# Attention in steps of two heads on eight cores of a Trainium2 chip, with allocations on multiples of 64 bytes

## The reference, cut to what matters

```python
q_nope, q_pe = q[..., :QK_NOPE_DIM], q[..., QK_NOPE_DIM:]      # 128 and 64
q_pe = rope(q_pe, positions)
k_pe = rope(k_rope[:, :, None, :], positions)                  # shared across heads
s = jnp.einsum('bqhd,bkhd->bhqk', qi, k).astype(jnp.float32) * scale   # over 192
s = jnp.where(mask[None, None], s, -jnp.inf)
p = jax.nn.softmax(s, axis=-1).astype(v.dtype)
return jnp.einsum('bhqk,bkhd->bqhd', p, v)
```

## Time and profile before

| | us |
|---|---|
| median of 3 runs | 2039.23 (2038.88 to 2039.92) |
| profiled execution, own time | 2044.05 |
| its span, slowest core (5) | 2042.5 |
| spans of the even cores | 1987.8 to 1994.6 |
| spans of the odd cores | 2033.2 to 2042.5 |
| core 5: TensorE busy | 1921.9 (94%) |
| VectorE / ScalarE / GpSimd busy | 1022.4 / 740.6 / 174.7 |
| DMA, mean | 86 GB/s |

### The profile page before, as it was taken

How to read it: one execution, slowest core, us unless ns; L and a number is a source line. 1 busy time by engine, 2 the same in 40 slices (tenths; PEclk the granted TensorE clock), 3 DMA queues, 4 the chain that set the end, 5 groups by cost and what they waited for, 6 DMA issues and landing times.

```text
span 2042.5 us, 26214 instructions; the slowest of 8 cores (1987.8 to 2042.5 us)
## 1 busy us (share of the span) xinstructions
PE 1921.9 (94%) x8362; PEld 788.1 (39%) x8362; DVE 1022.4 (50%) x1632; ACT 740.6 (36%) x1255; POOL 174.7 (9%) x332
## 2 busy tenths in 40 slices
PE   5999999989999999999999989999998998799996
PEld 1344544434444444444333433333343222244442
DVE  2265551463523426665565465665655575433335
ACT  3221232264321014543545333455533573311113
POOL 0021111100000100010000000110110000011110
PEclk8899999999999999999999999999999798899998
DMA  8186787744432322554222433553363001344542
GB/s 203 32 158 128 147 161 136 168 132 109 109 56 44 57 49 30 102 109 85 44 43 31 85 81 95 96 87 69 53 125 102 1 1 43 97 71 75 77 65 96
DMA packets 94686, 176.40 MB, mean 86 GB/s; under 512 B 25680, under 2 KB 46544, under 8 KB 93392
## 3 DMA queue, kind: packets, MB, share of 16 engines
q0 software_dynamic: 47232, 100.36, 31.7%
q1 hardware_dynamic: 47312, 74.26, 11.5%
HBM read 255.78 MB, written 19.14 MB: 135 GB/s over the span
## 4 chain that ended last, share of the span: by engine, by line
PE 85%; ACT 5%; DVE 5%; issue 3%; DMA 2%; SPq 1%; DVEq 0%; ACTq 0%; POOL 0%; POOLq 0%
PE ps L398 85%; ACT arena L402 4%; DVE arena L416 2%; DVE arena L406 2%; DMA arena<-wd 1%; ACT L402 1%; DMA arena<-smallc 1%; SPq L224 0%; DMA arena<-w_moR 0%; SPq L430 0%; ACTq L208 0%; DVEq L208 0%; ACT arena L422 0%; DVEq L175 0%; DVE arena L424 0%
## 5 line engine op out<-in xcount | busy, mean ns | idle before, releaser
L398 PE MATMUL ps<-arena 128*128 128x512 bf16 (+3 forms) x8362 | 1921.9, 381 | 107.2 <-DVE arena L406 35.7
L398 PEld LDWEIGHTS ps<-arena 128*128 128x128 bf16 (+1 forms) x8362 | 788.1, 98 | 1240.7 <-issue 444.4
L402 ACT ACTIVATE arena<-ps 128x512 bf16<-128x512 f32 (+2 forms) x677 | 390.7, 584 | 924.5 <-PE ps L398 868.3
L406 DVE TENSOR_TENSOR arena<-ps,arena 128x512 bf16<-128x512 f32 (+1 forms) x396 | 272.9, 691 | 694.1 <-PE ps L398 445.8
L416 DVE SCALAR_TENSOR_TENSOR arena<-ps,arena 128x512 f32<-128x512 f32 (+1 forms) x454 | 306.0, 689 | 143.8 <-PE ps L398 137.2
L406 DVE TENSOR_TENSOR arena<-arena 128x512 f32<-128x512 f32 (+10 forms) x456 | 274.7, 619 | 92.0 <-ACT arena L402 57.7
L402 ACT ACTIVATE arena<-arena 128x512 bf16<-128x512 f32 (+2 forms) x417 | 246.8, 624 | 177.8 <-PE ps L398 71.8
L416 DVE SCALAR_TENSOR_TENSOR arena<-arena 128x512 bf16<-128x512 f32 (+2 forms) x236 | 160.2, 728 | 55.9 <-ACT arena L402 36.9
L430 POOL DMA_DIRECT2D arena<-wgu x110 | 58.3, 530 | 1328.2 <-PE ps L398 1293.6
L430 POOL DMA_DIRECT2D arena<-wd x160 | 85.4, 535 | 455.4 <-PE ps L398 455.4
L422 ACT CAST arena<-ps 128x256 bf16<-128x256 f32 (+1 forms) x94 | 44.1, 477 | 114.0 <-PE ps L398 110.1
(11 more groups left out here) (15 smaller groups left out, 17.4 us busy)
## 6 DMA issues: line engine op xcount, KB each, us to landing
arena<-wgu POOLq DMA_DIRECT2D x110, 512.0 KB, 5.2
arena<-wd POOLq DMA_DIRECT2D x160, 160.0 KB, 3.3
arena<-win_s SPq DMA_DIRECT2D x46, 256.0 KB, 3.2
arena<-x SPq DMA_DIRECT2D x16, 512.0 KB, 5.5
arena<-x SPq DMA_DIRECT2D x8, 1024.0 KB, 11.3
arena<-wo_s SPq DMA_DIRECT2D x24, 256.0 KB, 2.6
arena<-xk_s SPq DMA_DIRECT2D x24, 256.0 KB, 2.6
arena<-vo_s SPq DMA_DIRECT2D x24, 256.0 KB, 2.7
```

Of the source, the lines that this page charges most:

```text
L398: S.add("pe", lambda e: e.matmul(out, lhsT=lhsT, rhs=rhs, start=start, stop=stop), reads, writes, cost=c)
L402: S.add("act", lambda e: e.activation(out=out, in_=in_, func=func, **kw), reads, writes, cost=0.17 + cols(out) * 0.00085, table=table)
L406: S.add(eng, lambda e: e.tensor_tensor(out=out, in0=in0, in1=in1, op=op), reads, writes, cost=c)
```

## The change

`attn_g` takes two heads at a time. A step is now one key block for the pair: the two 128-row matmuls of the heads, each into its own bank, then their two 64-row matmuls right behind each other, the first on the lower and the second on the upper half of the rows; then both exps (and triangle products); `stage_b` does two products and two adds. `LOOK` is 2 steps of two heads instead of 3 of one. The score banks and the product banks are taken two at a time. There are 6 slots PT in both branches, two used per step. Both tails of a pair run one after the other, one step after the pair's last product. On early cores the slots and sums are laid out anew, and RC is the same tile as ACC. The planner's cost of a matmul with 64 rows becomes half the streaming time plus 0.1 us. `take` rounds each size up to 64 bytes, so that what lies behind SC is no longer displaced by 488 bytes but by 512. The diff, with unchanged lines left out:

```diff
-    def mm(out, lhsT, rhs, start, stop, reads, writes):
-        c = cols(out) * (4.0 if out is None or lhsT.dtype == F32 else 1.0) * 0.000419
+    def mm(out, lhsT, rhs, start, stop, reads, writes, share=1.0):
+        c = cols(out) * (4.0 if out is None or lhsT.dtype == F32 else 1.0) * 0.000419 * share + (0.1 if lhsT.shape[0] == 64 else 0.0)
...
-        at[0] += nbytes
+        at[0] += -(-nbytes // 64) * 64
...
-    NPT = 6 if late else 5
+    NPT = 6
...
-        o_pt, o_acc, o_rc, o_ol = AW + 8 * K, AW + 13 * K, AW + 17 * K, AW + 21 * K
-        at[0] = max(at[0], AW + 25 * K)
+        o_pt, o_acc, o_rc, o_ol = AW + 8 * K, AW + 16 * K, AW + 16 * K, AW + 20 * K
+        at[0] = max(at[0], AW + 24 * K)
...
-    RC = [tile(("rc", i), o_rc + 2 * K * i, 2 * K) for i in range(2)]
+    RC = [tile(("rc" if late else "acc", i), o_rc + 2 * K * i, 2 * K) for i in range(2)]
...
-    LOOK = 3
+    LOOK = 2
...
-        seq = [(h, kb) for h in range(4) for kb in range(nk)]
+        seq = [(p, kb) for p in range(2) for kb in range(nk)]
...
-            b = yield from pa.get()
-            mm(ps[:, b, n0:512], KVN[:, ks], QA[:, h, n0:512], True, False, [BKVN[kb // 4], BQA[h]], [BPS[b]])
-            mm(ps[:, b, n0:512], KR[pr, ks], QPE[pr, h // 2, n0:512], False, True, [BKR[kb // 4], BQPE[h // 2]], [BPS[b]])
-            act(pt[:, n0:512], ps[:, b, n0:512], AF.Exp, [BPS[b]], [ptb], scale=sc_attn)
-            pa.put(b)
...
+            bs = yield from pa.get(2)
+            for e, b in enumerate(bs):
+                mm(ps[:, b, n0:512], KVN[:, ks], QA[:, 2 * p + e, n0:512], True, False, [BKVN[kb // 4], BQA[2 * p + e]], [BPS[b]])
+            for e, b in enumerate(bs):
+                pr = slice(64 * e, 64 * e + 64)
+                mm(ps[:, b, n0:512], KR[pr, ks], QPE[pr, p, n0:512], False, True, [BKR[kb // 4], BQPE[p]], [BPS[b]], share=0.5)
+            info[i] = []
+            for b in bs:
+                pt, ptb = PT[cnt["pt"] % NPT]
+                cnt["pt"] += 1
+                act(pt[:, n0:512], ps[:, b, n0:512], AF.Exp, [BPS[b]], [ptb], scale=sc_attn)
+                pa.put(b)
...
             if kb == 0:
-                pv[h] = yield from pa.get()
+                pv[p] = yield from pa.get(2)
+            for e in range(2):
+                pt, ptb, n0 = info[i][e]
+                b = pv[p][e]
+                mm(ps[:, b, n0:512], CTR[:, kb * 128:(kb + 1) * 128], pt[:, n0:512], kb == 0, kb == nk - 1, [BCTR[kb // 4], ptb], [BPS[b]])
+                acc, accb = ACC[e]
+                if kb == 1:
+                    p0, p0b, _ = info[i - 1][e]
+                    if n0:
+                        cp(acc[:, 0:n0], p0[:, 0:n0], [p0b], [accb])
+                    tt(acc[:, n0:512], p0[:, n0:512], pt[:, n0:512], ALU.add, [p0b, ptb], [accb])
...
-        def tail(h):
...
+        def tail(p):
+            for e in range(2):
+                rc, rcb = RC[e]
+                acc, accb = ACC[e]
...
-                    tails.append((k + 3, seq[k][0]))
+                    tails.append((k + 1, seq[k][0]))
```

More of the change, by code:

```diff
@@ L1000, in attn_g @@
         nk = 4 * (t + 1)
-        seq = [(h, kb) for h in range(4) for kb in range(nk)]
+        seq = [(p, kb) for p in range(2) for kb in range(nk)]
         pv, info, tails = {}, {}, collections.deque()
         def stage_a(i):
-            h, kb = seq[i]
+            p, kb = seq[i]
             n0 = max(0, kb - 4 * t) * 128
-            pt, ptb = PT[cnt["pt"] % NPT]
-            cnt["pt"] += 1
             ks = slice(kb * 128, (kb + 1) * 128)
-            pr = slice(64 * (h % 2), 64 * (h % 2) + 64)
-            b = yield from pa.get()
-            mm(ps[:, b, n0:512], KVN[:, ks], QA[:, h, n0:512], True, False, [BKVN[kb // 4], BQA[h]], [BPS[b]])
-            mm(ps[:, b, n0:512], KR[pr, ks], QPE[pr, h // 2, n0:512], False, True, [BKR[kb // 4], BQPE[h // 2]], [BPS[b]])
-            act(pt[:, n0:512], ps[:, b, n0:512], AF.Exp, [BPS[b]], [ptb], scale=sc_attn)
-            pa.put(b)
-            if kb >= 4 * t:
-                tt(pt[:, n0:n0 + 128], pt[:, n0:n0 + 128], TRI, ALU.mult, [ptb, BTRI], [ptb])
-            info[i] = pt, ptb, n0
+            bs = yield from pa.get(2)
[10 more added lines that the diff above has]
+                pa.put(b)
+                if kb >= 4 * t:
+                    tt(pt[:, n0:n0 + 128], pt[:, n0:n0 + 128], TRI, ALU.mult, [ptb, BTRI], [ptb])
+                info[i].append((pt, ptb, n0))
@@ L1020, in stage_b @@
         def stage_b(i):
-            h, kb = seq[i]
-            pt, ptb, n0 = info[i]
+            p, kb = seq[i]
             if kb == 0:
-                pv[h] = yield from pa.get()
[L1025 to L1034, removed]
@@ new lines, in stage_b @@
+            for e in range(2):
[8 more added lines that the diff above has]
+                    tt(acc[:, n0:512], p0[:, n0:512], pt[:, n0:512], ALU.add, [p0b, ptb], [accb])
+                elif kb > 1:
+                    tt(acc[:, n0:512], acc[:, n0:512], pt[:, n0:512], ALU.add, [accb, ptb], [accb])
@@ new lines, in tail @@
+        def tail(p):
+            for e in range(2):
+                rc, rcb = RC[e]
+                acc, accb = ACC[e]
+                b = yield from pa.get()
+                mm(ps[:, b, :], ONES32, acc, True, True, [BONES32, accb], [BPS[b]])
+                act(rc, ps[:, b, :], AF.Ln, [BPS[b]], [rcb])
+                pa.put(b)
+                act(rc, rc, AF.Exp, [rcb], [rcb], scale=-1.0)
+                tt(OL[:, 2 * p + e, :], ps[:, pv[p][e], :], rc, ALU.mult, [BPS[pv[p][e]], rcb], [BOL[2 * p + e]])
+                pa.put(pv[p][e])
```

## The result

The changed kernel takes 1958.7 us (median), before 2039.1: ratio 0.961 (0.9583 to 0.9637), 80 us less. Its profiled execution took 1959.5 us with a span of 1957.9. A ratio is that of a kernel to the kernel before on the same chip, with its 95% interval; 0.001 of it is 2 us. A difference of two ratios is uncertain by the root of the sum of the squares of the two half intervals, and a time given for it has that uncertainty.

What follows compares the result with a forecast made beforehand. TensorE bounds the slowest odd cores, together with VectorE where tile 7 attends alone. Terms 35 + 32 + 12 - 12 = 67 us gave 1977 for the profiled execution, 1972 us against the median, range 1952 to 2008.

Steps and rivals of the forecast that it cites:

- (a): Late cores' attention: two adjacent 64-row matmuls need one way in and out instead of two, 35 us gained.
- (b): Late cores' attention: a pair's two 64-row matmuls run at the same time, 32 us gained.
- (c): Matmuls outside attention: operands aligned to 64 bytes stream faster, 12 us gained, expected 11 to 15, lower bound 0.
- (e): Attention's pair steps: joint tails, narrow steps, slot waits and PSUM stalls lose 12 us, from 5 to 25.
- rival 1: 64-row pairs: the second weight load isn't hidden, 0.09 us per pair, 15 us off the overlap, 1987 us; chance 0.18.
- rival 2: 64-row pairs: no overlap at all, only one way in and out saved, 2004 us; chance 0.17.
- rival 3: 64-row pairs: changing row half costs like a change of height, 0.32 us, 2021 us; chance 0.05.
- (d): VectorE and ScalarE per pair: alternating sums give VectorE 1.22 us instead of 1.73, so TensorE bounds the lone stretch.
- The late first add: Start of each pair's row sum: the first add waits for step 3's exp, 4 us lost after half is covered.
- (f): Planner: new 64-row cost totals 0.415 per pair instead of 0.429, order and filler hardly shift, 0 us.
- Rival 4: Mixed stages: attention keeps missing its pair of PSUM banks, 99 us lost against 79 gained, 2060 us; chance 0.06.
- The even cores: Even cores: they gain too and end likelier at 1950 us, near 1974 at worst, so don't set the end.

Runs made afterwards that it cites:

- experiment 3: Changed kernel with each head's 64-row matmul right behind its own 128-row matmul, so no two are adjacent: ratio 0.9882.
- experiment 4: Changed kernel with both adjacent 64-row matmuls of a pair on the lower half of the rows: ratio 0.9735, 1985 us.
- experiment 1: Kernel before with only allocations rounded up to 64 bytes: ratio 0.9965.
- experiment 7: Changed kernel with a false dependency that makes every row-sum add wait for the one before: ratio 0.9752.
- experiment 8: Changed kernel with the 64-row matmuls apart and a false dependency chaining the adds of both sums: ratio 0.9869.
- experiment 10: Changed kernel with a step's triangle products ordered behind the adds of the same turn instead of ahead: ratio 0.9556, 1949.9 us.
- experiment 9: Kernel before with the 64-byte rounding and LOOK = 4 instead of 3 on late cores: ratio 0.9903.
- experiment 6: Changed kernel with eight probability slots instead of six, RC sharing ACC's place on late cores: ratio 0.9606, 1961.4 us or 1958.7 us by the text's pairing.
- experiment 11: Changed kernel with triangle products behind the adds, the planner's old cost, and row sums started by a copy of block 0: ratio 0.960.
- experiment 5: Changed kernel with the planner's old cost of a 64-row matmul: ratio 0.9568.
- experiment 12: Changed kernel with triangle products behind the adds and eight probability slots, RC in HN's place on late cores: ratio 0.9618.

## Why the prediction was right, point by point

The forecast was 1972 (1952 to 2008), the result 1958.7: direction and mechanism right, the gain 67 forecast and 80 measured. The terms are further off than their sum: (a) to (c) came out 17 us lower than forecast and (e) 29 higher, so part of how near the total came is luck. By terms:

| term | forecast | measured | from |
|---|---|---|---|
| (a) one way in and out less | 35 | 30 | experiments 3 and 4 |
| (b) overlap | 32 | 25 | experiment 4 and the change |
| (c) addresses | 12 | 7 (2 to 12) | experiment 1 |
| (e) losses of the new steps | -12 | about +17 | what is left, experiments 1 and 3 |
| sum | 67 | 79 | |

The measured terms lie between kernels that follow each other from before to after, so their sum must be the whole. Each of (a) and (b) is uncertain by 10 or 11 us, (e) by 10.

**(a)** was read from one period and three paces, and the trace after has it: two head-steps have one way in and one way out. The 5 us short are within the uncertainty.

**(b)** was taken near the lower of two bounds, on an argument. The measured difference of starts is 3 to 4 ns. The Trainium skill, TensorE: Matmul & The Clock Gate, Measured speedup vs the span model, gives about 4 ns of issue per tile; this trace agrees, with 3 to 4. Its measured 3.07 for four row tiles, from which I worked out rival 1 by the page, doesn't carry over to two tiles here: the pair streams in the time of one. Rivals 1 to 3 are out (0.09 and 1.38, 1.51, 1.61 against the measured 0.004 and 1.29). The overlap saves 34 us of streaming, and 25 (uncertain by 10) arrived.

**(c)** The mechanism is shown, at the numbers forecast. I took every nanosecond of TensorE as one of the end, and counted the cross-attention matmuls too, which stream the aligned HN; 7 of 12 arrived, and in the changed kernel 1 with an uncertainty of 9.

**(d)** was right, and more important than I made it. I entered it as a check that VectorE doesn't bind, worth nothing in the sum. Experiments 7 and 8 show that 29 us of the gain stand on it: had the heads kept one chain of sums, VectorE would have held the lone stretch at 1.73. The Trainium skill, TensorEngine Tiling (Array Packing), PSUM Bottleneck, says that tiling speeds up TensorE and not the evacuation of PSUM, which may become the bottleneck. Experiment 7 shows a bound behind TensorE, 1.73 per pair, but it is made by the row sums in SBUF and not by reading PSUM; in the changed kernel the bound did not move, since VectorE starts an op each 0.60 us and not each 0.69.

**(e)** is the term that failed, by sign. The losses exist: the exps of the narrow steps wait 1.02 us each for VectorE, 3.3 us in the lone stretch that experiment 10 gets back. But the same restructuring has a gain that the prediction set to nothing: scores and product of a head are now four head-steps apart instead of three. I read LOOK = 2 as a smaller number. Experiment 9 gives the old kernel the same distance, and with it 13 us; how much of the 17 it makes here, and how much goes with the clock, stays open. The late first add, which I priced at 4 us, doesn't show in experiments 6 and 11.

**(f)** The cost change didn't bring gain; the old cost is as good or 9 us better.

**Rival 4,** banks: TensorE stays busy for 168.19 of 170 us in the mixed stage. It didn't happen. **The even cores** I expected near 1950; they end at 1938 to 1944. Their stage of small attentions does more matmuls in the same time, at an even lower busy share (215.64 of 280, 847 matmuls against 812 in the earlier trace rows):

```profile
760.00:1040.00 280.00, 215.64 (x847) 79.85 (x845) 141.73 (x259) 113.94 (x207) 2.64 (x5) 0.88 0.22 59
```

What stays open: how the plan's shifts of 9 to 13 us come about (experiments 5 and 12) and why the shorter chain of experiment 6 brings nothing, where most of experiment 10's gain comes from, and how much of the low clock at the start of before's lone stretch belongs to the kernel rather than to that execution.

## What to carry to other kernels

Put matmuls of 64 rows next to each other on opposite row halves, each with its own bank as here (one bank for both wasn't tried): each pair then costs one streaming time and one change of height, and the trace before already shows the price of the change as the excess of a step's period over its matmuls' paces. Before counting such a gain, look at the period of the next engine in the same step, and at whether its ops wait for the one just before: here the same adjacency was worth 24 us with a dependent sum and 55 us with two alternating ones. When a step changes its size, convert the look-ahead, the number of slots and the order within VectorE's queue to the new unit: the first and the last moved the end by some 10 us each, and too few slots for the new step put a wrong block into the row sums.

## What the runs showed of the hardware that I hadn't expected

- A change between 128 and 64 rows costs about 0.10 us on each side (starts 0.312 and 0.319 apart instead of 0.216), but a 64-row matmul right behind another adds none: on the same rows it starts some 0.22 us later, on the other half 3 to 4 ns later.
- 512-column bf16 matmuls whose moving operand starts 40 bytes past a multiple of 64 run at 0.2173 us, aligned ones at 0.2158; VectorE's ops are not affected (their adds take 689 ns on either side of the change).
- VectorE ops that don't depend on the one before start 0.60 us apart though each record is 0.69 long; dependent ones 0.86 to 0.87. Waits that were already met added no time there.
